# A two-layer trunk on one core: token areas for the hidden activations, and a new order of work at the start, in the attention, in HGRN and in the tail

## The reference

```python
x = x + 0.5 * swiglu(rmsnorm(x, ffn1_norm[i]), ffn1_w_in[i], ffn1_w_out[i])
h = rmsnorm(x, mix_norm[i])
x = x + (s5_mixer if i == 0 else hgrn2_mixer)(h, ...)
x = x + cross_attend(rmsnorm(x, xattn_norm[i]), mem_k[i], mem_v[i], w_q[i], w_o[i])
x = x + 0.5 * swiglu(rmsnorm(x, ffn2_norm[i]), ffn2_w_in[i], ffn2_w_out[i])
...
x = rmsnorm(x, final_norm)
```

## Time and profile before

| | |
|---|---|
| median of 3 runs | 2386.51 us (2385.75 to 2387.01) |
| profiled execution | 2385.19 us |
| its span | 2383.4 us |
| granted TensorE clock, mean | 0.999 |
| TensorE busy | 2351.9 us (99%) |
| VectorE, ScalarE, GpSimd busy | 54%, 37%, 25% |
| chain that ended last: TensorE's share | 90% |
| weight matmuls (three products), the two costliest lines of that chain | 51% and 25% |

### The profile page before, as it was taken

How to read it: one execution, slowest core, us unless ns; L and a number is a source line. 1 busy time by engine, 2 the same in 40 slices (tenths; PEclk the granted TensorE clock), 3 DMA queues, 4 the chain that set the end, 5 groups by cost and what they waited for, 6 DMA issues and landing times.

```text
span 2383.4 us, 50169 instructions
## 1 busy us (share of the span) xinstructions
PE 2351.9 (99%) x21068; PEld 2289.6 (96%) x21068; DVE 1291.9 (54%) x1903; ACT 872.1 (37%) x1398; POOL 605.3 (25%) x591
## 2 busy tenths in 40 slices
PE   8999999999999999999999999999999999999999
PEld 8999999889979999999999999999998969999998
DVE  6654643964575543446543344577777666443442
ACT  4422333543233331232333233267774233221322
POOL 3779957431103000004111010442122103000003
PEclk9999999999999999999999999999999999999999
DMA  5456445563563333333543333333332653333332
GB/s 161 131 156 152 118 122 162 178 177 106 152 237 93 95 95 91 98 103 94 160 116 110 104 104 111 91 99 101 101 108 75 211 186 89 97 93 93 97 101 85
DMA packets 483707, 289.19 MB, mean 121 GB/s; under 512 B 22289, under 2 KB 466962, under 8 KB 482514
## 3 DMA queue, kind: packets, MB, share of 16 engines
q1 hardware_dynamic: 477856, 280.66, 39.8%
q0 software_dynamic: 560, 1.84, 0.6%
q10 hardware_dynamic: 5122, 4.25, 0.5%
HBM read 258.86 MB, written 27.85 MB: 120 GB/s over the span
## 4 chain that ended last, share of the span: by engine, by line
PE 90%; POOL 3%; DVE 3%; ACT 1%; DMA 1%; issue 1%; ACTq 0%; DVEq 0%; SPq 0%; POOLq 0%
PE lin L2918 51%; PE lin L2923 25%; PE mis L2414 3%; PE mis L2553 1%; POOL sTmp L720 1%; PE lin L2501 1%; POOL sGe L721 1%; PE lin L2885 1%; POOL sGe L719 1%; POOL sFe L721 1%; PE mis L2716 0%; PE lin L2666 0%; PE lin L2534 0%; PE mis L2534 0%; DMA raw<-in_xattn_w_kv_dram 0%
## 5 line engine op out<-in xcount | busy, mean ns | idle before, releaser
L1777 DVE TENSOR_TENSOR w_lo<-raw,w_hi 128x1024 fp32r<-128x1024 f32 (+1 forms) x322 | 463.2, 1439 | 300.0 <-ACT w_hi L1307 299.5
L1307 ACT ACTIVATE w_hi<-raw 128x1024 fp32r<-128x1024 f32 (+1 forms) x328 | 364.8, 1112 | 303.8 <-PE lin L2923 247.5
L2918 PE MATMUL lin<-a_rear,w_hi 128*128 128x264 f32 x3552 | 455.7, 279 | 0.0
L2918 PE MATMUL lin<-a_front,w_hi 128*128 128x256 f32 x3552 | 451.6, 279 | 1.1 <-DVE a_rear L1790 0.7
L2918 PEld LDWEIGHTS lin<-a_rear,w_hi 128*128 128x128 f32 x3552 | 432.9, 188 | 0.0
L2918 PEld LDWEIGHTS lin<-a_front,w_hi 128*128 128x128 f32 x3552 | 424.5, 188 | 4.5 <-issue 1.8
L2923 PE MATMUL lin<-a_rear,w_lo 128*128 128x264 f32 x1776 | 245.1, 278 | 0.0
L2923 PE MATMUL lin<-a_front,w_lo 128*128 128x256 f32 x1776 | 240.7, 277 | 2.0 <-DVE w_lo L1777 2.0
L2325 DVE SCALAR_TENSOR_TENSOR xT<-lin,xT 128x520 f32<-128x520 f32 (+1 forms) x88 | 61.6, 700 | 332.4 <-PE lin L2923 331.1
L1040 POOL TENSOR_TENSOR acc<-xT 128x520 f32<-128x520 f32 x8 | 12.2, 1519 | 870.4 <-DVE xT L2325 842.2
L2923 PEld LDWEIGHTS lin<-a_rear,w_lo 128*128 128x128 f32 x1776 | 223.8, 188 | 0.0
(11 more groups left out here) (495 smaller groups left out, 3404.6 us busy)
## 6 DMA issues: line engine op xcount, KB each, us to landing
raw<-in_ffn_w_in_dram SPq DMA_DIRECT2D x176, 512.0 KB, 3.8
raw<-in_ffn_w_out_dram SPq DMA_DIRECT2D x64, 704.0 KB, 4.6
kc<-in_cache_mem_k_dram SPq DMA_DIRECT2D x32, 512.0 KB, 7.1
vc<-in_cache_mem_v_dram SPq DMA_DIRECT2D x16, 1024.0 KB, 8.9
raw<-in_hg_w_in_dram SPq DMA_DIRECT2D x32, 512.0 KB, 4.2
raw<-in_xattn_w_kv_dram SPq DMA_DIRECT2D x16, 512.0 KB, 4.4
raw<-in_s_w_glu_dram SPq DMA_DIRECT2D x16, 512.0 KB, 4.0
raw<-in_xattn_w_q_dram SPq DMA_DIRECT2D x16, 512.0 KB, 4.4
```

Of the source, the lines that this page charges most:

```text
L1307: act.activation(w_hi[:, j, 0:kt, :], raw[:, j, 0:kt, :], ACT.Copy).then_inc(hi_ready, 1)
L1777: dve.tensor_tensor(low_weights(n, j), raw[:, j, 0:kt, :], w_hi[:, j, 0:kt, :].bitcast(F32), ALU.subtract).then_inc(lo_ready, 1)
L2918: pe.matmul(lpart(j, half), high[:, k, :], (x_lo if u else x_hi)[half][:, k, :], start=start and u == 0 and k == 0, stop=False)
```

## The change

- **Areas.** g_hi and g_lo, for glu and xo, lie as a and f do: fronts tile behind tile (1024 bytes each), then rears (1152 bytes each). hg_out keeps h. `token_pair` writes 512 tokens of a tile as two pieces. S5's output is written in six parts (HIDDEN) instead of eight tiles.
- **Start.** The first weights are loaded ahead of row tiles 2 and 3, and split by ScalarE ahead of the norm's copies. The 16 scale rows of ffn1 are turned alone; the others after the first chunk, into another bank. Row tile 3 and the samples are turned inside the first product. Rear upper and front lower products alternate. The squares of tile 3 move from ScalarE to VectorE.
- **S5.** FU waits for its own U group.
- **Attention.** Both score groups of head 0 are issued between xq's chunks. The list, the banks and the places of `weighted` change; W is copied by ScalarE; pP is two buffers; all eight samples' values are multiplied in one go before O(3,0).
- **HGRN.** In one chunk (h = 1) all w_lo products come last. The sample rows T are turned by two transposes instead of two fp32 matmuls on four columns. The states are made earlier in the first and last head. `projected` ends in another order, and ScalarE splits the second pair's weights ahead of the first gain.
- **Tail.** The last chunk finishes its front half first; row tiles 0 and 1 get their sums and scale from it, tile 0 is turned inside the chunk. Each token is summed once.

```diff
+    g_all = [at(f"g_all{e}", [P, KD * (FRONT + 2 * REAR) // 4], F32R, o) for e, o in enumerate((o_hid, o_lo))]
+    g_hi, g_lo = ((t[:, 0:KD * TF].rearrange("p (k n) -> p k n", k=KD),
+                   t[:, KD * TF:KD * HTILE // 4].rearrange("p (k n) -> p k n", k=KD)[:, :, 0:TR]) for t in g_all)
...
+    def token_pair(e, k):
+
+        step = (KD * FRONT + k * (REAR - FRONT)) // 4
+        return g_all[e][:, k * TF:k * TF + 2 * step].rearrange("p (a n) -> p a n", a=2)[:, :, 0:TF]
...
-    made = [("B", (b, 0), "dve") for b in range(NS)]
-    XA_EARLY = {4: range(0, 3), 5: range(3, 6), 6: range(6, 8)}
+    made = [("B", (b, 0), "dve") for b in range(NS)] + [("S", (0, 0), "act"), ("S", (0, 1), "act")]
+    XA_EARLY = {4: range(0, 3), 5: range(3, 6), 6: range(6, 9), 7: range(9, 10)}
     XA_MAIN = len(made)
-    made += [("S", (0, 0), "act"), ("S", (0, 1), "act"), ("B", (0, 1), "dve"), ("B", (1, 1), "dve")]
-    made += [("S", (1, 0), "act"), ("B", (2, 1), "dve"), ("P", (0, 0), "act"), ("P", (0, 1), "act")]
-    made += [("S", (1, 1), "act"), ("B", (3, 1), "dve"), ("O", (0, 0), "dve"), ("O", (0, 1), "dve")]
+    made += [("B", (0, 1), "dve"), ("S", (1, 0), "act"), ("B", (1, 1), "dve"), ("P", (0, 0), "act"), ("P", (0, 1), "act")]
+    made += [("S", (1, 1), "act"), ("B", (2, 1), "dve"), ("B", (3, 1), "dve"), ("O", (0, 0), "dve"), ("O", (0, 1), "dve")]
     made += [("S", (2, 0), "act"), ("B", (4, 1), "dve"), ("B", (5, 1), "dve"), ("P", (1, 0), "act"), ("P", (1, 1), "act")]
     made += [("S", (2, 1), "act"), ("B", (6, 1), "dve"), ("O", (1, 0), "dve"), ("O", (1, 1), "dve")]
-    made += [("S", (3, 0), "act"), ("B", (7, 1), "dve"), ("P", (2, 0), "act"), ("P", (2, 1), "act"), ("T", 0, "act")]
-    made += [("S", (3, 1), "act"), ("O", (2, 0), "dve"), ("W", 0, "dve"), ("O", (2, 1), "dve")]
+    made += [("S", (3, 0), "act"), ("B", (7, 1), "dve"), ("P", (2, 0), "act"), ("P", (2, 1), "act")]
+    made += [("S", (3, 1), "act"), ("T", 0, "act"), ("O", (2, 0), "dve"), ("O", (2, 1), "dve"), ("W", 0, "act")]
     made += [("P", (3, 0), "act"), ("P", (3, 1), "act"), ("O", (3, 0), "dve"), ("V", 0, "dve"), ("O", (3, 1), "dve")]
-    WEIGHTED = {("B", (0, 1)): 0, ("B", (1, 1)): 1, ("S", (1, 1)): 2, ("O", (0, 0)): 3, ("B", (5, 1)): 4, ("O", (1, 0)): 5,
-                ("T", 0): 6, ("O", (2, 1)): 7}
-    XA_BANKS = [q % 4 for q in range(XA_MAIN)] + [(4, 5, 0, 1, 2, 3)[q % 6] for q in range(len(made) - XA_MAIN)]
+    WEIGHTED = {("B", (0, 1)): [0, 1], ("S", (1, 1)): [2], ("O", (0, 0)): [3], ("B", (5, 1)): [4], ("O", (1, 0)): [5],
+                ("T", 0): [6], ("O", (2, 0)): [7]}
+    XA_BANKS = [q % 4 for q in range(XA_MAIN)] + [(4, 5, 2, 3, 0, 1)[q % 6] for q in range(len(made) - XA_MAIN)]
     XAG = [Groups(made, xa[l]["fill"], xa[l]["void"], banks=XA_BANKS) for l in range(DEPTH)]
...
+    HIDDEN = [(0, 0, 6, 1), (0, 6, 7, 1), (1, 0, 3, 1), (0, 7, 8, 1), (1, 3, 6, 2), (1, 6, 8, 2)]
...
+                if t == 2:
+                    column, src = weights(0, 0, 0)
+                    sp.dma_start(raw[:, 0, 0:KD, :], src[:, :, bass.ds(column, P)]).then_inc(raw_arrived[0], 16)
                 sp.dma_start(xin[:, t, :], i_["x_prompt"][0, t * P:(t + 1) * P, :]).then_inc(rows_in[t], 16)
             sp.dma_start(xsin[:], i_["x_sample"].rearrange("b o d -> (b o) d")).then_inc(xs_loaded, 16)
...
+            split(0, 0, 0)
...
-            split(0, 0, 0)
...
-                        if (j == 0 or not first or r is None) and not (name == "hg_out" and first and j == 0):
+                        if (j == 0 or not first or r is None) and not (name == "hg_out" and first):
...
+                        if name == "xq" and last and j == 1:
+                            attend(layer, range(XA_MAIN - 2, XA_MAIN))
...
+                        if name == "hg_out" and first and j == 0:
+                            split(p + 1, 0, chunk_after(n, 1, last))
                         if after is not None and is_out(name):
                             act.wait_ge(used[j], p + 1)
                             gain_hi(2 * i + j, NORM_ROW[after])
...
+            rows_evacuate(2)
+            split(0, 0, 0)
+            rows_evacuate(3)
...
+            row_squares(3).then_inc(squares_done, 1)
+            dve.wait_ge(vec_tr, 2)
+            dve.tensor_copy(vec[:, 2 * KD:NVEC], mis[:, 2, 2 * KD:NVEC]).then_inc(vec_done, 1)
...
+                done = hidden_before(number("glu"))
+                for half, first, end, inc in HIDDEN:
+                    done += inc
+                    dve.wait_ge(h_hi_done, done)
+                    dve.tensor_tensor(g_lo[half][:, first:end, :], u32[:, first:end, COLS[half]],
+                                      g_hi[half][:, first:end, :].bitcast(F32), ALU.subtract)\
+                        .then_inc(h_lo_done if half else front_lo_done, end - first)
...
-                        dve.tensor_copy(hO[:, e, SEQ:NT], hg_bank(q)[:, 0:NS]).then_inc(hg["void_dve"], 1)
+                        dve.tensor_copy(hO[:, e, SEQ:NT], hg_bank(q)[:, 0:2 * P:P // 4]).then_inc(hg["void_dve"], 1)
...
+                    if h == HH:
+                        states(g)
...
+                    if 0 <= d < HH and h != HH:
+                        hidden_lo(d)
+                    if h == 1:
+                        states(g)
                     if 0 < h < HH:
                         values(p, b)
...
+                    if 0 < g < HH - 1:
+                        states(g)
...
+            def last_tile(half):
+                cols = COLS[half]
+                dve.wait_ge(chunk_done, 2 * ALL_PAIRS + half)
+                dve.scalar_tensor_tensor(out=xT[:, KD - 1, cols], in0=lpart(1, half), scalar=0.5, in1=xT[:, KD - 1, cols],
+                                         op0=ALU.mult, op1=ALU.add).then_inc(used[1], 1)
+                dve.wait_ge(squares_done, NORMS)
+                dve.wait_ge(y_gained, KD + 2 * half)
+                dve.tensor_tensor(acc[:, cols], acc[:, cols], t2[:, cols], ALU.add).then_inc(y_scale, 1)
...
+            def vectors_turn():
+
+                pe.wait_ge(vrows_loaded, 16 * 8)
+                pe.wait_ge(in_evac["dve"], 4)
+                pe.transpose(mis[:, 2, 0:NVEC], vrows[0:NVEC, :], ident[0:NVEC, 0:NVEC]).then_inc(vec_tr, 1)
+
+            for t in range(2):
+                rows_turn(t)
+            pe.wait_ge(gain_loaded, 16)
+            pe.transpose(lin[:, 0, 0, 0:2 * KD], vrows[0:2 * KD, :], ident[0:2 * KD, 0:2 * KD]).then_inc(vec_tr, 1)
+            rows_turn(2)
             pe.wait_ge(vec_done, 1)
...
-                        if u == 2 * MH - 2:
-                            sample_values(layer, range(0, 6))
...
-                            sample_values(layer, range(6, NS))
+                            sample_values(layer, range(NS))
...
-                        if a % 8 == 0:
-                            for u in (6, 7):
-                                G.emptied_of(pe, "U", a + u)
+                        G.emptied_of(pe, "U", a)
...
-                        ins = pe.matmul(bank[:, 4 * f:4 * (f + 1)], sRow[:, f, :], ident[:, 0:P:32], start=True, stop=True)
+                        ins = pe.transpose(bank[:, f * P:(f + 1) * P], sRow[:, f, :], ident[:])
...
-                        chunk(p + 1, 1, False)
+                        chunk(p + 1, 1, False, h == 1)
...
-                projected([(1, 5), (0, 6), (1, 6), (0, 7), (1, 7)])
+                projected([(1, 5), (0, 6), (0, 7), (1, 6), (1, 7)])
...
+                    x_hi, x_lo = (tuple(t[:, :, cols] for cols in COLS) for t in (h_hi, h_lo)) if name == "hg_out" else (g_hi, g_lo)
...
-                        product(0, w_hi, x_hi, 0, start=True)
+                        product(0, w_hi, x_hi, 0, start=True, ks=range(FRONT_TILES))
+                        rows_turn(3)
+                        samples_turn()
+                        product(0, w_hi, x_hi, 0, ks=range(FRONT_TILES, KD))
                         pe.wait_ge(lo_ready, 1)
                         product(0, w_lo8, x_hi, 0)
-                        product(0, w_hi, x_hi, 1, start=True)
-                        product(0, w_hi, x_lo, 0, stop=True)
+                        for k in range(KD):
+                            product(0, w_hi, x_hi, 1, start=True, ks=(k,))
+                            product(0, w_hi, x_lo, 0, stop=True, ks=(k,))
                         product(0, w_lo8, x_hi, 1)
+                        vectors_turn()
                         pe.wait_ge(hi_ready, 2)
...
+                    elif low_last:
+                        for half in range(2):
+                            for u in range(2):
+                                high_weights(half, u, range(kt), True)
+                        pe.wait_ge(lo_ready, 2 * p + j + 1)
+                        for half in range(2):
+                            ins = low_weight_tiles(half, range(kt))
...
+                def last_chunk(p):
+
+                    pe.wait_ge(hi_ready, 2 * p + 2)
+                    wait(pe, used[1], p)
```

(28 more changed lines are left out.)

283 lines of the change are left out of this document (151 added, 132 removed).

## The result

The changed kernel takes 2366.3 us (median of 4 runs, 2364.88 to 2368.55) against 2386.19 beside it: a ratio of 0.9917, 95% interval 0.9901 to 0.9932, so 19.9 us less. 2367.7 was forecast, 18.8 less. The profiled execution took 2364.88 us; its span is 2363.1, 20.3 under that of before.

What follows compares the result with a forecast made beforehand. TensorE, busy in 99% of the span, was taken to bound the kernel. The terms, 1.3 + 0.5 + 4.5 + 3.8 + 0.35 + 1.85 + 0.7 + 3.6 + 2.2 = 18.8 us, gave 2386.5 - 18.8 = 2367.7; range 2363.0 to 2373.5.

Steps and rivals of the forecast that it cites:

- the idle sum: Whole kernel: the prediction called itself wrong if TensorE's idle sum, 31.5 us before, stayed above 22 us.
- Token areas: glu and both xo stages: reading by areas saves 2.9 ns on each of 1536 matmuls, 4.5 us.
- Rival D: glu and xo: the areas slow the stream; at 132 ns a matmul the kernel takes 2393.9 us; chance 0.01.
- Attention: Both layers: early scores and a new order remove TensorE's waits, about 1.9 us per layer, 3.8; range 1 to 3 each.
- rival A: Attention, start, S5, HGRN: removed waits become waits for VectorE, attention giving only 1 us; 2372.5 us; chance 0.21.
- HGRN (a): One HGRN head: the 1.54 us wait for w_lo goes, but 1.2 returns at the next chunk; gain 0.35 us.
- (b): HGRN's T groups: transposes instead of fp32 matmuls save 0.23 us in each of eight heads, 1.85 us.
- (c): HGRN's last head: states made ahead of two VectorE operations remove 0.7 us of idle for hS.
- (d): Start of hg_out: 2.0 us of idle goes and the clock stays at 1.00, another 1.6; together 3.6 us.
- The start: Kernel's beginning: scale-row wait goes and products interleave, so norm sums come 1.3 us earlier; range 0 to 2.5.
- S5: FU groups wait only for their own U copy, removing 0.99 us of idle; gain 0.5 us, between 0 and 1.0.
- The tail: Kernel's end: token sums done once and first row tiles sent during the last chunk; gain 2.2 us, range 1 to 3.

Runs made afterwards that it cites:

- experiment 1: Changed kernel with glu's input again in rows of 520 tokens (2176 bytes from tile to tile), both xo stages keeping the areas: 2371.06 us.
- experiment 10: Changed kernel with hg_out's upper part written by areas and the first three output row tiles sent together when the third is scaled: 2370.85 us.
- 2 and 3: Changed kernel with glu's input in rows of 2304 and of 2080 bytes from tile to tile: 2373.04 and 2371.66 us.
- experiment 7: Changed kernel with head 0's two score groups issued with the main part of the attention again, not between xq's last chunks: 2367.04 us.
- experiment 8: Changed kernel with three edits undone: S5's FU wait, HGRN's T by transposes, the low weights last in head 1: 2369.11 us.
- experiment 4: Changed kernel with ScalarE making the weights of hg_out's second pair behind the first gain again: 2369.02 us.
- 11: Changed kernel with the order of hg_out's last products undone and the first chunk of HGRN's head 2 also multiplying its low weights last: 2367.11 us.
- experiment 9: Changed kernel with both hg_out orders (last products, ScalarE) undone and row tile 0 turned behind the last chunk: 2371.50 us.
- experiments 5 to 8: Changed kernel once more, 2367.02 us; changed kernel with first weights queued between row tiles 2 and 3, 2366.23 us; then experiment 7 and experiment 8.

## Why the prediction was right, point by point

- **The base, TensorE as the bound**, held: TensorE is busy 99% in both, and every gain is read on its timeline. Of the signs of being wrong, the idle sum was close: 21.9 us, with 22 named.
- **Token areas (4.5)**: 2.1 + 1.2 + 1.1 = 4.4, and experiment 1 shows that glu's layout does it, experiment 10 the same for single front groups; which property of the layout it is stays open (2 and 3). The step that read the pace from starts, and took f as witness, carried the largest term. By the prediction's reading of the rule of the Trainium skill, "SBUF — State Buffer", Specifications (TRN2), contiguous columns would go at one pace in either layout and the term would be 0; 88.81 and 90.88 us for the same 768 matmuls say otherwise. Rival D falls too: the pace is 115.6 ns, not above 130.
- **Attention (3.8, range 2 to 6)**: 2.6 + 2.2 = 4.8. The size was in the range; the first step of its mechanism failed: "the chain runs beside 48 matmuls" is true and worth nothing (experiment 7). The walk also had VectorE late by 0.7 at the last key group, of which the trace shows nothing, and rival A, which left attention 1 us, falls there. The risk of the late value transfer did not come true: the block of 128 matmuls at 703.81 runs through.
- **HGRN (a), 0.35**: 0.2, and the waits that took the place are those for hS (0.79) and the next w_lo (0.45), 1.24 in all, as the slack in the earlier trace rows said. **(b), 1.85**: 0.32 per head where 0.23 was read off the row's length, but only in the six heads ahead of hg_out; 0 in the last two, where TensorE waits for ScalarE's hgS and VectorE's sS whatever T takes. Six times 0.32 is 1.9. **(c), 0.7**: about right where T is as in before, 0.6 in experiment 8; the 0.7 of idle for hS is gone. But (c) and the last two T groups, 1.16 together in the sum, do not add up: the stretch from the first hg_out product to the last hgS turn is 0.5 shorter than in before, with 0.54, 0.30, 0.28 and 0.15 us of waits for hgS, hO and sS where before had 0.40 and 0.20 beside the 0.70 for hS.
- **(d), 3.6**: the profile gave it (the lead goes from 11.2 to 14.8), but the reason was incomplete in the first part and failed in the second. ScalarE's order alone is worth 1.4 (experiment 4) and the products' order 0.65 (11); together they are the 2.0 of idle. "Without the gap it should stay" said nothing of the reverse: with the same 1.97 us gap the clock stayed at 1.00 in experiment 9. The 1.6 us for the clock was in the profile of before and not in that run, so part of this term is the luck of one profile. How often before loses it at this place is open. That it loses clock somewhere is common: beside experiments 5 to 8 the mean granted clock was 0.998 or 0.997 in all nine executions of before, and 0.999 to 1.000 in the five of the changed kernel.
- **The start, 1.3**: the mechanism was right, but "Were it 1.3 us late", with a gain of 0, was written as the end of a range where it is the usual case (the wait for tile 2 was 0.9 to 2.6 us in eleven profiles), and lateness is not what takes the gain: with waits of 1.43 to 1.58 the start gained 1.7 to 2.2, with waits from 0.88 up it gained -0.7 to 0.4 in the eight where the clock was low. The prediction had no term for the clock here. The sum took one profile's worth, and so did the result.
- **S5, 0.5**: 0.4 in the table. The FU edit is worth 0.3 to 1.1 where the clock stays up (experiment 8), inside the range of 0 to 1.0 or just above; a clock that falls in this stretch, as in six profiles, takes more than that back.
- **The tail, 2.2**: 2.2, for the reason given: it is gone when the first tiles are held back (experiment 10).

The profile gained 20.3 us where the sum had 18.8: attention gave 1.0 more and TensorE's earlier first work 0.7, the other terms differ by 0.6 at most and nearly cancel. That the median came out so close (19.9) is in part luck. Some 3 us of it, the start's gain and the 1.6 for the clock in (d), hang on how the clock stood in the executions compared. The prediction named the clock only in (d), and its reason there failed.

## What to carry to other kernels

Read the pace of a stream from start to start over whole blocks, and compare stages that differ only in layout: less than 3 ns a matmul over 1536 matmuls was 4.4 us here, and no view of waits shows it. A wait removed in a chain of three engines can move to the next of them, so cost it by the slack behind it (0.33 us in the earlier trace rows, 0.2 gained). Where a gain hangs on when a transfer lands or on the clock's state, one profile is one draw: look at the same place in the profiles of several variants before putting a number on it, and read the length of equal instructions beside the row of the clock.
